# Moving the attention's value products to another burst of small matrix products, and a gate product to another quarter

## The reference

```
h = rmsnorm(x, norm_gain); proj = h @ w_in                    # 2048 -> 6528 columns
# group 1: 16 heads of RWKV-7: S <- S*w + sa*b + v*k, y = S r, over the tokens
# group 2: 16 heads of sliding-window attention, blocks of 128 tokens, window 128
s = einsum(q, kw) * 64**-0.5 - slope * dist                   # keys of this block and the one before
prob = softmax(concat(s, sink))[..., :-1]
o = einsum(prob, vw);  y_attn = o * silu(g_attn)              # "values": this product is moved
mix = concat(y_rwkv * silu(g_rwkv), y_attn)
x = x + mix @ w_out;   out = rmsnorm(x, final_gain)
```

## Time and profile before

| | |
|---|---|
| median of 3 runs | 1822.35 us (1821.75 to 1823.31) |
| the profiled execution | 1822.79 us, of which the program's span is 1820.8 us |
| PE busy | 1803.7 us, 99% of the span |
| DVE busy | 1248.6 us, 69% |
| ACT busy | 832.0 us, 46% |
| POOL busy | 476.8 us, 26% |
| mean granted clock of PE | 0.998 |

### The profile page before, as it was taken

How to read it: one execution, slowest core, us unless ns; L and a number is a source line. 1 busy time by engine, 2 the same in 40 slices (tenths; PEclk the granted TensorE clock), 3 DMA queues, 4 the chain that set the end, 5 groups by cost and what they waited for, 6 DMA issues and landing times.

```text
span 1820.8 us, 37389 instructions
## 1 busy us (share of the span) xinstructions
PE 1803.7 (99%) x14519; PEld 1479.8 (81%) x14519; DVE 1248.6 (69%) x2255; ACT 832.0 (46%) x1725; POOL 476.8 (26%) x1093
## 2 busy tenths in 40 slices
PE   9999999999999999999999999999999999999997
PEld 7778888888888888888888888888888788888886
DVE  5876777777767688667777777776778854345445
ACT  7544445454535355444453545353535553242335
POOL 0014233241505060142432415050606060100110
PEclk9999999999999999999999999999999999999999
DMA  8633333333333345433333333333323543466546
GB/s 302 198 92 91 92 97 86 97 92 91 98 92 99 84 108 166 114 86 92 96 87 96 92 96 95 91 100 83 106 78 107 166 138 103 130 202 202 167 126 231
DMA packets 200289, 217.09 MB, mean 119 GB/s; under 512 B 98864, under 2 KB 104112, under 8 KB 199472
## 3 DMA queue, kind: packets, MB, share of 16 engines
q1 hardware_dynamic: 190032, 197.19, 37.6%
q10 hardware_dynamic: 10080, 17.51, 3.4%
HBM read 192.61 MB, written 22.02 MB: 118 GB/s over the span
## 4 chain that ended last, share of the span: by engine, by line
PE 95%; DVE 3%; ACT 1%; issue 1%; DMA 0%; ACTq 0%; SPq 0%; DVEq 0%
PE psum L1404 70%; PE psum L1389 3%; PE psum L1679 3%; PE psum L1681 3%; PE psum L1680 3%; PE psum L1522 2%; PE psum L1462 2%; PE psum L1490 1%; PE psum L1671 1%; PE psum L1555 1%; PE psum L1635 1%; DVE w_lo L929 1%; PE psum L1642 1%; PE psum L1424 1%; PE psum L1623 1%
## 5 line engine op out<-in xcount | busy, mean ns | idle before, releaser
L1404 PE MATMUL psum<-x_hi,w_hi 128*128 128x512 f32 x1888 | 763.5, 404 | 2.5 <-DVE x_lo L938 2.2
L1404 PE MATMUL psum<-x_hi,w_lo 128*128 128x512 f32 x1888 | 738.5, 391 | 0.0
L1404 PE MATMUL psum<-x_lo,w_hi 128*128 128x512 f32 x1888 | 736.3, 390 | 0.0
L929 DVE TENSOR_TENSOR w_lo<-w_raw,w_hi 128x512 fp32r<-128x512 f32 x522 | 368.2, 707 | 393.2 <-ACT w_hi L665 362.6
L665 ACT ACTIVATE w_hi<-w_raw 128x512 fp32r<-128x512 f32 x522 | 326.1, 628 | 665.9 <-PE psum L1404 596.7
L1404 PEld LDWEIGHTS psum<-x_hi,w_hi 128*128 128x128 f32 x1888 | 355.2, 188 | 87.6 <-DVE w_lo L929 9.9
L1404 PEld LDWEIGHTS psum<-x_hi,w_lo 128*128 128x128 f32 x1888 | 354.6, 188 | 77.2
L611 POOL TENSOR_TENSOR sub_t<-sub_l,sub_io 128x60 f32<-128x60 f32 (+24 forms) x496 | 192.5, 388 | 850.1 <-DMA sub_l<-scratch_L 812.5
L1404 PEld LDWEIGHTS psum<-x_lo,w_hi 128*128 128x128 f32 x1888 | 355.7, 188 | 66.9 <-issue 0.5
L613 POOL TENSOR_TENSOR sub_io<-sub_io,sub_t 128x60 f32<-128x60 f32 (+24 forms) x496 | 207.1, 418 | 38.8
L1679 PE MATMUL psum<-w_hi,x_hi 128*128 128x512 f32 x256 | 100.3, 392 | 1.4 <-DVE w_lo L929 1.2
(11 more groups left out here) (276 smaller groups left out, 2092.8 us busy)
## 6 DMA issues: line engine op xcount, KB each, us to landing
w_raw<-in_w_in SPq DMA_DIRECT2D x348, 256.0 KB, 2.7
w_raw<-in_w_in ACTq DMA_DIRECT2D x60, 256.0 KB, 2.8
w_raw<-in_w_out SPq DMA_DIRECT2D x60, 256.0 KB, 2.7
w_raw<-in_w_rows SPq DMA_DIRECT2D x50, 256.0 KB, 2.8
stage<-in_w_rows SPq DMA_DIRECT2D x30, 256.0 KB, 2.8
sub_l<-scratch_L SPq DMA_DIRECT2D x16, 384.0 KB, 4.1
stage<-in_x_t SPq DMA_DIRECT2D x20, 256.0 KB, 4.2
stage<-scratch_MIX SPq DMA_DIRECT2D x19, 256.0 KB, 3.7
```

The lines of the kernel that those rows point to most:

```text
L929: nc.vector.tensor_tensor(w_lo[gq % SPLIT][:], w_raw[raw_of(gq)[0]][:], w_hi[gq % SPLIT][:].bitcast(F32), ALU.subtract).then_inc(w_ready, 1)
L1404: mm = nc.tensor.matmul(psum[:, bank_of(s)], wt[gq % SPLIT][:, cols], xx[:, c], start=(c == 0 and wt is w_hi and xx is x_hi), stop=(c == K ...
```

## The change

For the 14 intervals for which `values_with_state(i)` is true (all but 6 and 14), the values' products leave step 16 and stand at step 19 between G's products and the state's. Inside `values`, for all intervals, the half with 64 rows now comes first. DVE's `attended` goes from step 18 to 20 and SP's store of sa from step 20 to 21. DVE's gt waits for the values' products (`o_full`), since it overwrites what they read. The gate's product on DVE goes from step 22 to 23 (all intervals but 7 and 15).

```diff
+def values_with_state(i):
+
+    return i % PAIRS != PAIRS - 2
@@ sync, recurrence
-                    if at == 20:
+                    if at == (21 if values_with_state(i) else 20):
                         sp.wait_ge(mixa_ready, i + 1)
@@ vector, channels
-                    if at == (25 if last_of_half(j) else 22):
+                    if at == (25 if last_of_half(j) else 23):
                         dve.wait_ge(ga_sig, j + 1)
@@ vector, transition
                     dve.sem_inc(mt_ready, 1)
+                    dve.wait_ge(o_full, i + 1)
@@ vector, recurrence
-                    if at == 18:
+                    if at == (20 if values_with_state(i) else 18):
                         attended(i)
@@ tensor, values
-                            add(b, sub, 0, vs[:, b + 1] if sub else va[:, own - 1, kv], 0, b + sub == 0, False)
-                            add(b, sub, 1, va[:, own, kv] if sub else vs[:, b + 1], 2, b + sub == 0, False)
+                            add(b, sub, 0, vs[low, b + 2] if sub else va[low, own, kv], 1, b + sub == 0, False)
+                            add(b, sub, 1, va[high, own - 1, kv] if sub else vs[high, b], 1, b + sub == 0, False)
...
-                            add(b, sub, 0, vs[low, b + 2] if sub else va[low, own, kv], 1, False, True)
-                            add(b, sub, 1, va[high, own - 1, kv] if sub else vs[high, b], 1, False, True)
+                            add(b, sub, 0, vs[:, b + 1] if sub else va[:, own - 1, kv], 0, False, True)
+                            add(b, sub, 1, va[:, own, kv] if sub else vs[:, b + 1], 2, False, True)
@@ tensor, recurrence, step 16
-                        values(i)
+                        if not values_with_state(i):
+                            values(i)
@@ tensor, recurrence, step 19
                         mm.then_inc(mg_full, 1)
+                        if values_with_state(i):
+                            values(i)
```

## The result

| | before | changed |
|---|---|---|
| median of 16 runs, us | 1822.38 (1821.4 to 1823.44) | 1825.86 (1822.82 to 1828.54) |
| ratio to before, 95% interval | | 1.0018 (1.0011 to 1.0024) |
| the profiled execution / its span, us | 1822.79 / 1820.8 | 1827.4 / 1825.4 |
| first product of interval 0's recurrence (step 1), us | 116.5 | 115.4 |

The kernel became slower by 3.5 us, 0.18%, and its runs scatter over 5.7 us where those of before scatter over 2.0.

What follows compares the result with a forecast made beforehand. PE, busy 99% of the span, was taken as the bound. Bursts -4.2, corner waits +4.7, DVE and SP 0 gave +0.5 us: 1823.3 for the profiled execution, median 1822.9, range 1818.0 to 1827.0.

Steps and rivals of the forecast that it cites:

- Taking the values' products out, 2.16, and putting them in, 1.86 us: PE, steps 16 and 19: 2.16 us leaves, 1.86 returns, saving 0.30 per interval, 4.2 us for 14.
- The corner waits, 4.7 us: PE at the corner: waits for xt in intervals 1, 2, 5, 8 and 15, 4.7 us in all.
- `under` has time to spare: PE at `under`: x_back lands in time after the shift, except in interval 8, where the corner waits anyway; no cost.
- The price of a wait is its length: PE at the corner: late landings counted at their lateness, 4.2 us, plus 0.1 handoff for each of five.
- The landings look like chance: DMA into xt: apart from intervals 15 and 7, late landings scatter by chance; another execution should again give 4.7 us.
- VectorE's moves cost nothing: DVE, steps 20 and 23: `attended`, the wait before gt and the gate's product fit in, costing 0 us.
- The sum, +0.5 us and no measurable change: Whole kernel: bursts -4.2, corner +4.7, DVE and SP 0, so +0.5 us; within 0.2% (3.6 us), chance 0.68.
- my rival with waits nearly everywhere: PE at the corner: xt late in nearly all 14 intervals, mean wait 0.7 us; +5.6 us, 1828.0; chance 0.10.

Runs made afterwards that it cites:

- the short inverse: The changed kernel with POOL's inversion loop cut by four steps, against the kernel before: 1818.23 us, ratio 0.9979; the kernel before with the same cut: 1821.68.
- the gate alone: The kernel before with only DVE's gate product moved from step 22 to 23: 1822.26 us, ratio 1.0001.
- the run with the late inverses: The changed kernel with ten more small products at the end of POOL's loop, so that xt lands later: 1882.0 us, ratio 1.0324 to the kernel before.

## Why the prediction was right or wrong, point by point

- *Taking the values' products out, 2.16, and putting them in, 1.86 us.* Right to 0.01 us in interval 3. The Trainium skill's rule (TensorEngine Tiling, Key Properties) that a change of mode drains the engine holds at the size that the rows gave it, not of a whole product: the short inverse gained 3.5 to 3.9 us, not 6.2. No run changed the tile shapes alone.
- *The corner waits, 4.7 us.* Nearly right in sum, 5.4 us, and in place, intervals 2, 5, 8 and 15. That the sum fits is in part luck, for single terms do not: interval 1 was in time instead of 0.7 late, 2 waited 2.3 instead of 0.6, 15 waited 0.8 instead of 1.3.
- *`under` has time to spare.* Mis-sized: 1.2 us, in intervals 2 and 8, where I counted nothing because the corner would wait anyway. Waits at two steps do not always lie over one another: in interval 2 PE waited 0.6 for sub_io and then 2.3 for xt.
- *The price of a wait is its length.* This step failed, and is the larger half of the error in the profiled execution (3.1 of the 5.2 us by which its body passed the forecast's +0.5): the clock dropped after the waits of two intervals. Nothing in the rows of before showed it, since PE has no such wait there once it is under way, and I priced no rival for it.
- *The landings look like chance.* Wrong. They belong to places, with chance on top: of the intervals with a code transfer in the wrong place two thirds were late. What POOL makes of it is uneven. In interval 2 sub_l landed 2.3 us later than in interval 3 (5.4 and 3.0 after the issue), and POOL ended 2.6 us later; in the same interval of the kernel before, sub_l landed 1.5 us later than in interval 3 and POOL ended 0.4 later. The last operation of its inversion, intervals 2 and 3, 44.75 and 42.13 us after their first products (at 287.43 and 377.63):

```profile
332.18 0.73 POOL L620 COPY sub_io<-sub_io 128x256 f32<-128x256 f32 x1 [0.17 <-POOL sub_io L618]
...
419.77 0.66 POOL L620 COPY sub_io<-sub_io 128x256 f32<-128x256 f32 x1 [0.17 <-POOL sub_io L618]
```

- *VectorE's moves cost nothing.* Right: the gate alone is 1.0001, and no wait on VectorE appears in the run without waits for DMAs.
- *The sum, +0.5 us and no measurable change.* The measured +3.5 lies inside the range and within the 0.2% (0.18%), and that is in part luck: the range had no term for the clock, and the profiled execution, 1827.4 with a body longer by 5.7 us, lies outside it. In size this is near my rival with waits nearly everywhere (+5.6), without being it: few intervals wait, and longer. The mean wait was to be measurably slower from 0.56 us; it was 0.47 in that execution, and the clock did the rest.

## What to carry to other kernels

Before work is moved off a stretch of the bounding engine, list what lands in that stretch and by how much, for every repetition and not for a typical one; here 0.30 us were gained per interval and 2.16 us of cover given away. Price a wait of a busy TensorE above its length once it nears two microseconds: in the run where nearly every interval waited, 44.4 us of waits cost 16.5 us more. Where an exchange pays only in the undisturbed repetitions, choose them one by one: nine of 14 gained 2.0 us where 14 lost 3.5. Look for instruction transfers beside a DMA that is late always at the same place of the program.

## What the runs showed of the hardware that was not expected

- The granted clock fell to 0.5 for 3.4 us after waits of 0.6 and 2.3 us one quarter apart amid full work (1.5 us lost), and did not after waits of 1.4 us and less. In the run with the late inverses waits of 0.5 and 1.7 us were enough once and one of 2.8 us was not, so the length of the wait alone does not decide.
- Where a 16 KB transfer of TensorE's instructions began 1.4 to 3.2 us behind the issue of a 384 KB transfer, this landed 0.6 to 2.4 us later than the usual 3.0 in two cases of three, and the late places moved when the instructions were moved. The Trainium skill (Runtime: NRT & Kernel Launch, Instruction fetch mechanics) says that instruction blocks of 16 KiB are streamed by DMA and the cost is mostly hidden. For the engine's own stream that agrees with the traces, which show no wait of it; the cost here falls on another queue's data. How the two collide inside the DMA engines the runs don't show.
- GpSimd's loop of 31 steps passes a late start on unevenly: 2.3 us became 2.6 at its end, 1.5 us became 0.4. I read it as waiting for VectorE's operations at the same memory, but no run tests that.
